# A Fourier transform folded over mirrored positions and computed in turns of the fill-in bank during attention

## What is computed

```python
def fourier_mix(u):
    b, n, _ = u.shape
    uh = u.astype(F32).reshape(b, n, FOURIER_HEADS, HEAD_DIM)
    y = jnp.fft.fft2(uh, axes=(1, 3), norm='ortho').real
    return y.reshape(b, n, GROUP_WIDTH).astype(u.dtype)
...
        y = jnp.concatenate([
            gated_short_conv(a_v, a_b, a_c, conv_w[layer]),
            multiscale_pool(p_in, pool_w[layer], pool_scale[layer]),
            neighborhood_attention(q, k, v, kc, vc, na_rpb[layer]),
            fourier_mix(f_in),
        ], axis=-1)
        x = x + g1 * (y @ w_out[layer])
```

## Time and profile before

| what | value |
|---|---|
| median of three runs | 584.47 us (584.3 to 585.58) |
| the profiled execution | 587.96 us, of which its span 585.8 us |
| busy, PE | 548.4 us (94%) |
| busy, DVE | 447.2 us (76%) |
| busy, ACT | 321.8 us (55%) |
| busy, POOL | 155.8 us (27%) |
| HBM traffic | 160.15 MB read, 17.33 MB written |

### The profile page before, as it was taken

How to read it: one execution, slowest core, us unless ns; L and a number is a source line. 1 busy time by engine, 2 the same in 40 slices (tenths; PEclk the granted TensorE clock), 3 DMA queues, 4 the chain that set the end, 5 groups by cost and what they waited for, 6 DMA issues and landing times.

```text
span 585.8 us, 7662 instructions
## 1 busy us (share of the span) xinstructions
PE 548.4 (94%) x2733; PEld 416.7 (71%) x2733; DVE 447.2 (76%) x592; ACT 321.8 (55%) x399; POOL 155.8 (27%) x141
## 2 busy tenths in 40 slices
PE   1789999999999999979999899999999999999995
PEld 1344874677766877857688688888888888877772
DVE  1347688534576465477899899999999999999867
ACT  4440132354442922255586586676876677866624
POOL 5000743132230510020871321233312333210060
PEclk9799999999999999988999899999999999999998
DMA  8999995759521740149979999999999999999565
GB/s 288 390 371 318 376 379 189 234 158 401 216 73 56 267 145 37 46 153 396 323 291 392 383 345 392 393 392 393 391 388 391 390 390 379 380 383 358 199 223 208
DMA packets 88902, 173.92 MB, mean 297 GB/s; under 512 B 5399, under 2 KB 18907, under 8 KB 88749
## 3 DMA queue, kind: packets, MB, share of 16 engines
q1 hardware_dynamic: 82722, 155.43, 73.9%
q10 hardware_dynamic: 2780, 9.99, 4.2%
q0 software_dynamic: 3376, 8.18, 3.9%
HBM read 160.15 MB, written 17.33 MB: 303 GB/s over the span
## 4 chain that ended last, share of the span: by engine, by line
PE 76%; DMA 8%; DVE 7%; ACT 4%; issue 3%; SPq 1%; POOL 0%; DVEq 0%; ACTq 0%; POOLq 0%
PE psum L897 6%; PE psum L1271 4%; PE psum L1273 4%; PE psum L1244 4%; PE psum L1272 4%; PE psum L1245 4%; PE psum L1246 4%; PE psum L905 4%; PE psum L1255 3%; PE psum L1256 3%; PE psum L1254 3%; DMA w<-in_moe_w 3%; PE psum L942 3%; DMA ada<-in_ada_w 3%; PE psum L944 3%; PE psum L943 3%
## 5 line engine op out<-in xcount | busy, mean ns | idle before, releaser
L2245 DVE TENSOR_TENSOR w_lo<-w,w_hi 128x2048 fp32r<-128x2048 f32 x32 | 72.9, 2282 | 1.2 <-ACT w_hi L1670 1.2
L2234 DVE TENSOR_TENSOR w_lo<-w,w_hi 128x1024 fp32r<-128x1024 f32 (+2 forms) x30 | 68.6, 2292 | 0.0
L1661 ACT CAST w_hi<-w 128x2048 fp32r<-128x2048 f32 x30 | 57.3, 1911 | 15.7 <-PE psum L1256 14.4
L1670 ACT CAST w_hi<-w 128x2048 fp32r<-128x2048 f32 x32 | 60.3, 1917 | 7.2 <-issue 4.1
L2228 DVE TENSOR_TENSOR w_lo<-w,w_hi_a 128x2048 fp32r<-128x2048 f32 (+1 forms) x30 | 51.7, 1760 | 3.2 <-ACT w_hi_a L1649 2.8
L1271 PE MATMUL psum<-w_hi,heT_hi 128*128 128x512 f32 x120 | 50.1, 417 | 0.8 <-DVE w_lo L2245 0.8
L763 POOL COPY idx<-idx 128x1 int32 x12 | 10.4, 870 | 141.5 <-PE psum L1217 141.5
L1852 DVE SCALAR_TENSOR_TENSOR rows<-ada,cc,rows 128x512 f32<-128x512 f32 x48 | 39.5, 825 | 10.6 <-DMA ada<-in_ada_w 9.1
L1273 PE MATMUL psum<-w_hi,heT_lo 128*128 128x512 f32 x120 | 47.5, 396 | 0.0
L1272 PE MATMUL psum<-w_lo,heT_hi 128*128 128x512 f32 x120 | 47.2, 393 | 0.0
L1245 PE MATMUL psum<-w_lo,xgT_hi 128*128 128x512 f32 x120 | 46.8, 390 | 0.0
(11 more groups left out here) (368 smaller groups left out, 1265.1 us busy)
## 6 DMA issues: line engine op xcount, KB each, us to landing
w<-in_moe_w SPq DMA_DIRECT2D x32, 2048.0 KB, 13.6
w<-in_moe_w SPq DMA_DIRECT2D x32, 1024.0 KB, 13.6
ada<-in_ada_w SPq DMA_DIRECT2D x12, 2048.0 KB, 18.7
win<-in_w_in SPq DMA_DIRECT2D x8, 1024.0 KB, 14.5
expert_rows<-ysb ACTq DMA_DIRECT2D x15, 512.0 KB, 6.4
expert_rows<-zero SPq DMA_DIRECT2D x1, 5120.0 KB, 21.4
wout<-in_w_out SPq DMA_DIRECT2D x4, 1024.0 KB, 4.9
x<-in_x SPq DMA_DIRECT2D x2, 1024.0 KB, 10.7
```

The source lines that it names most:

```text
L1670: act.copy(w2_hi[:, :, hs], w2_sb[b][:, :, hs]).then_inc(w2_hi_ok[half], 1)
L2234: v.tensor_tensor(w3_lo[b][:, ks, :], w3_sb[b][:, ks, :], w3_hi[:, ks, :], ALU.subtract).then_inc(w3_lo_ok, n)
L2245: v.tensor_tensor(w2_lo[b][:, :, hs], w2_sb[b][:, :, hs], w2_hi[:, :, hs], ALU.subtract).then_inc(w2_lo_ok[half], 1)
```

## The change

The transform is folded. POOL adds and subtracts mirrored positions once (sums for the cosines, differences for the sines), and then once or twice more, so that even and odd frequencies need only 65, 64, 128, 128 and 127 positions. Over channels PE then has ten matmuls with 128 columns, over positions ten that together have 1024 columns, 512 for each half of the 256 channels. They are done in five turns, where rounds 2 to 6 of the loop put a third half tile or nothing: turns 0 to 2 over channels, turns 3 and 4 over positions. Each turn uses bank 7, so it waits until the tile before is out, and the next tile waits until ACT has copied the turn's result. POOL joins the mirrored outputs into a buffer of their own (`yF`). The third half tiles move to rounds 0, 1 and 7, one half tile falls into round 8, and the pooling matmuls are put before the last `output`.

The quarters of `w_out` are loaded in the order k = 4,5; 6,7; 0,1; 2,3, and ACT rounds the first two in rounds 7 and 8; POOL forms the low parts of these two, DVE of the others. The first projection handles both halves of the first 128 tokens, first with k = 4, 6, 7, 0, 1, then with k = 5, 2, 3. One expert load (the first matrix of expert 1) is issued earlier on SP, after the last tile.

```diff
-        def more_fill(p):
-
-            return p % 2 == 0
+        FOURIER_AT = (2, 3, 4, 5, 6)
+
+        def third(p):
+
+            return p < 2 or p == NP_ - 1
+
+        HI_AT = [3, 4, 5, 6, 2, 7, 0, 1]
+
+        def wout_ks(i):
+
+            return slice(2 * (i ^ 2), 2 * (i ^ 2) + 2)
 
...
+            sp.wait_ge(ada_dve, 5)
+            sp.dma_start(dft_sb[:], dft_seq).then_inc(dft_in, 16)
...
+            load_first(moe_w1, w1_sb, 1, w1_in)
             sp.wait_ge(pool_ps, 2)
             sp.wait_ge(o_copied, 2)
             load_first_w2(1)
-            sp.wait_ge(fn_ok, 2)
-            load_first(moe_w1, w1_sb, 1, w1_in)
...
+            low_w(2)
+            low_w(3)
+
+            def both(dst_sum, dst_dif, a, b):
+
+                gp.tensor_tensor(dst_dif, a, b, ALU.subtract)
+                link(gp.tensor_tensor(dst_sum, a, b, ALU.add))
+
+            gp.wait_ge(pj_act, 2)
+            both(f_sum[:, :, 1:GW], f_dif[:, :, 1:GW], fT[:, :, 1:GW], fT[:, :, GW + 1:N][:, :, ::-1])
+            both(f_sum[:, :, 0:1], f_odd[:, :, 0:1], fT[:, :, 0:1], fT[:, :, GW:GW + 1])
+            both(f_sum[:, :, 1:P], f_odd[:, :, 1:P], f_sum[:, :, 1:P], f_sum[:, :, P + 1:GW][:, :, ::-1])
+            both(f_dif[:, :, 1:P], f_rest[:, :, 0:P - 1], f_dif[:, :, 1:P], f_dif[:, :, P + 1:GW][:, :, ::-1])
+            gp.tensor_tensor(f_half[:], f_sum[:, :, 0:HD], f_sum[:, :, HD + 1:P + 1][:, :, ::-1], ALU.subtract)
+            gp.tensor_tensor(f_sum[:, :, 0:HD], f_sum[:, :, 0:HD], f_sum[:, :, HD + 1:P + 1][:, :, ::-1], ALU.add
+                             ).then_inc(fold_ok, 1)
+            for n in range(4, len(FILL)):
...
+            def mirrored(up_, down, even, odd):
+
+                gp.tensor_tensor(up_, even, odd, ALU.add)
+                return gp.tensor_tensor(down, even, odd, ALU.subtract)
+
+            gp.wait_ge(fn_even, 2)
+            e4, e2, e1 = f_parts[:, :, 0:65], f_parts[:, :, 65:129], f_parts[:, :, 129:257]
+            o1, o2 = f_parts[:, :, 257:385], f_parts[:, :, 385:N]
+            mirrored(yF[:, :, 1:GW:2], yF[:, :, GW + 1:N:2][:, :, ::-1], e1, o1)
+            mirrored(yF[:, :, 2:GW:4], yF[:, :, GW + 2:N:4][:, :, ::-1], e2, o2[:, :, 0:127:2])
+            mirrored(yF[:, :, 4:GW:4], yF[:, :, GW + 4:N:4][:, :, ::-1], e4[:, :, 1:64], o2[:, :, 1:127:2])
+            gp.tensor_copy(yF[:, :, 0:GW + 1:GW], e4[:, :, 0:65:64]).then_inc(fn_copied, 1)
+
+            for i in range(2):
                 gp.wait_ge(wo_hi_ok, i + 1)
                 ks = slice(2 * i, 2 * i + 2)
-                gp.tensor_tensor(wout_lo[:, ks, :], wout[:, ks, :], wout_hi[:, ks, :], ALU.subtract).then_inc(wo_lo_gp, 1)
+                gp.tensor_tensor(wout_lo[:, ks, :], wout[:, ks, :], wout_hi[:, wout_ks(i), :], ALU.subtract
+                                 ).then_inc(wo_lo_gp, 1)
...
+            def fourier(i):
+
+                if i == 0:
+                    pe.wait_ge(consts_in, 112)
+                    pe.wait_ge(fold_ok, 1)
+                if i < 3:
+                    pe.wait_ge(pj_act, 4 + i)
+                    cos, sin = head_dft[:, 0:P], head_dft[:, P:2 * P]
+                    for h in range(2):
+                        mine = ([(f_sum[:, h, 0:HD + 1], cos), (f_half[:, h, :], cos)],
+                                [(f_odd[:, h, :], cos), (f_dif[:, h, 1:P + 1], sin)],
+                                [(f_rest[:, h, 0:P - 1], sin)])[i]
+                        for a, (w, c_) in enumerate(mine):
+                            n = w.shape[1]
+                            m = pe.matmul(bank[7][0:n, a * GW + h * P:a * GW + (h + 1) * P], w, c_,
+                                          start=True, stop=True)
+                    m.then_inc(fd_ok, 1)
+                    return
+                h = i - 3
+                pe.wait_ge(pj_dve, i - 2)
+                pe.wait_ge(fd_copied, 3)
+                pe.wait_ge(dft_in, 16)
+                for a, k, cols_ in ((0, 65, slice(0, 65)), (1, HD, slice(65, 129)), (2, P, slice(129, 257)),
+                                    (3, P, slice(257, 385)), (4, P - 1, slice(385, N))):
+                    m = pe.matmul(bank[7][:, cols_], f_freq[a][0:k, h * P:(h + 1) * P], dft_sb[0:k, cols_], start=True, stop=True)
+                m.then_inc(fn_ok, 1)
...
+                if p == NP_:
+                    pe.wait_ge(d_ok, 1)
+                    for h in range(2):
+                        pe.matmul(bank[2 + h][:], pw[:, h, :], dpool[:, h, :],
+                                  start=True, stop=True).then_inc(pool_ps, 1)
...
-                if more_fill(p):
+                if p in FOURIER_AT:
+                    fourier(FOURIER_AT.index(p))
+                elif third(p):
                     fill(nf)
                     nf += 1
-            while nf < 20:
-                fill(nf)
...
-            for t in range(NT):
-                for h in range(2):
-                    m = pe.matmul(bank[t][:, h * GW:(h + 1) * GW], fT[:, h, t * P:(t + 1) * P], head_dft[:],
...
-                        m = pe.matmul(bank[4 + h][:, cols_], fcs[:, t, h, part * P:(part + 1) * P],
...
+            def project_part(ks, high, low, turned):
+
+                for n in range(2):
+                    cc_ = slice(n * 512, (n + 1) * 512)
+                    tc = slice(0, P)
+                    for k in ks:
+                        if n == 0:
+                            pe.wait_ge(y_hi_ok, high[k][0])
+                            pe.wait_ge(wo_hi_ok, high[k][1])
+                        pe.matmul(bank[n][:], yT_hi[:, HI_AT[k], tc], wout_hi[:, k, cc_], start=(k == 4), stop=False)
+                    for k in ks:
+                        if n == 0:
+                            pe.wait_ge(*low[k])
+                        pe.matmul(bank[n][:], yT_hi[:, HI_AT[k], tc], wout_lo[:, k ^ 4, cc_], start=False, stop=False)
+                    for k in ks:
+                        if n == 0:
+                            pe.wait_ge(y_lo_ok, turned[k])
+                        m = pe.matmul(bank[n][:], yT_lo[:, k, tc], wout_hi[:, k, cc_], start=False, stop=(k == 3))
+                    if ks[-1] == 3:
+                        m.then_inc(wo_ok, 1)
 
             def project_first():
 
...
+                high = {4: (1, 1), 6: (2, 2), 7: (2, 2), 0: (3, 3), 1: (3, 3), 5: (5, 1), 2: (4, 4), 3: (4, 4)}
+                low = {4: (wo_lo_gp, 1), 5: (wo_lo_gp, 1), 6: (wo_lo_gp, 2), 7: (wo_lo_gp, 2),
+                       0: (wo_lo_ok, 1), 1: (wo_lo_ok, 1), 2: (wo_lo_ok, 2), 3: (wo_lo_ok, 2)}
+                turned = {4: 1, 6: 2, 7: 2, 0: 3, 1: 3, 2: 4, 3: 4, 5: 5}
+                project_part((4, 6, 7, 0, 1), high, low, turned)
+                project_part((5, 2, 3), high, low, turned)
...
             project_first()
-            project(1)
             project(2)
...
-                act.wait_ge(pj_dve, 4)
-                act.wait_ge(d_ok, 1)
-                act.wait_ge(stored, 16)
-                act.copy(wout_hi[:, 2 * i:2 * i + 2, :].rearrange("p k n -> p (k n)"),
+                act.wait_ge(*((fn_copied, 1), (fn_copied, 1), (pj_dve, 3), (pj_dve, 4))[i])
+                act.copy(wout_hi[:, wout_ks(i), :].rearrange("p k n -> p (k n)"),
...
+                    act.wait_ge(fn_ok, i - 2)
+                    act.wait_ge(d_ok, 1)
+                    act.copy(f_parts[:, i - 3, :], bank[7]).then_inc(fn_even, 1)
...
+                if p == NP_:
+                    high_wout(1)
...
+                if p in FOURIER_AT:
+                    fourier_copy(FOURIER_AT.index(p))
+                elif third(p):
+                    nf += 1
+                    if done < len(FILL) and nf >= 2 * (done + 1):
+                        tile_done(done)
+                        done += 1
+                if p == NP_ - 1:
+                    act.wait_ge(o_copied, 1)
+                    high_y(4, 1)
+                    high_wout(0)
+                    high_y(6, 2)
...
+            high_y(0, 2)
             high_wout(2)
+            act.wait_ge(pool_ok, 2)
+            high_y(2, 2)
+            act.wait_ge(o_copied, 2)
+            high_y(5, 1)
             high_wout(3)
...
+            late = {(3, 0): pool_pairs, (3, 1): pool_fours, (4, 0): pool_eights, (4, 1): lambda: pool_means(0),
+                    (5, 0): lambda: pool_means(1), (5, 1): lambda: (conv_in(0), pool_less()),
+                    (6, 0): lambda: conv(0), (6, 1): lambda: conv_in(1), (7, 0): lambda: conv(1),
+                    (7, 1): lambda: conv_out(0), (8, 0): lambda: conv_out(1)}
...
+            low_y(1, 4, 1)
+            low_y(2, 6, 2)
+            low_y(3, 0, 2)
+            low_wout(2)
+            head_pair(1)
+            low_y(4, 2, 2)
+            low_y(5, 5, 1)
+            low_wout(3)
...
+    seq = np.zeros((P, N))
+    seq[0:65, 0:65] = cos[0:65, 0:257:4]
+    seq[0:64, 65:129] = cos[0:64, 2:256:4]
+    seq[:, 129:257] = cos[0:P, 1:256:2]
+    seq[:, 257:385] = sin[1:P + 1, 1:256:2]
+    seq[0:127, 385:N] = sin[1:P, 2:256:2]
```

(36 more changed lines are left out.)

130 lines of the change are left out of this document (41 added, 89 removed).

## The result

The changed kernel takes 582.1 us (median of 7 runs, 581.39 to 583.82), the kernel before 586.88 (7 runs, 584.3 to 587.82; three of them are those of the table before, the four new ones took 586.88 to 587.82). The ratio of the means is 0.9931, with a 95% interval of 0.9908 to 0.9954: **faster, by 4.0 us (2.7 to 5.4)**, or 0.7%. A second measurement later gave 582.1 again, ratio 0.9943 (0.9922 to 0.9964). The profiled execution took 582.48 us, its span 580.2 us.

A forecast was written before the change was run, and what follows sets the result against it. PE, busy 94% of the span, was taken as the bound. Terms -5.9 - 3.0 - 2.1 + 5.1 + 1.5 = -4.4 us, from the median 584.47 to 580.1 us; range 576.5 to 582.8 us.

The forecast's parts named there:

- turns on PE: Ten channel matmuls at 2.45 us and a position part at 1.83 us added to PE, together 4.3 us.
- waits in the loop: PE's waits for ACT's two copies (0.81 + 0.68 us) and for DVE (1.5 us) covered by moved work: -3.0 us.
- Fourier rows gone: The old channel and position transforms removed from PE's tail: 3.45 + 6.72 = 10.17 us.
- old waits of the first part: Idle time in the old first projection part, 7.57 us where its matmuls need 5.46, all gone: -2.1 us.
- new waits: First projection part, after the last `output` ends (Z): PE idle 1.9 us for ACT and 3.2 for DVE, +5.1 us.
- clock: One stretch of PE at the lower clock level around the tail's new idle time: +1.5 us of 0 to 3.4.
- rival C: A longer stretch at the lower clock, or one more wait at seams without room: 582.1 us; chance 0.12.
- the prediction's own sign: Projection of the second 128 tokens starts 5.9 (at full clock) or 4.4 us earlier than 216.7, else the step is wrong.
- The hold: In the tail, POOL's work on `w_out` keeps DVE's low parts of yT from starting until Z + 1.6.
- Rival B: DVE isn't held by POOL in low yT: 2.0 of 3.2 us go, 576.6 us with the clock high; chance 0.12.
- Rival A: PE's clock stays high behind the tail's new gaps: -5.9 us, 578.6 us; chance 0.22.
- Nothing on POOL or in the loop became late: POOL's fold (6.6 us, 7 with waits) and joining (3.4 us), and the turns' new waits in the loop, costed at nothing.

The follow-up runs named there:

- pool_one_quarter: The changed kernel with DVE instead of POOL forming the low part of the second quarter of `w_out`: 579.61 us, ratio 0.9897 to the kernel before.

## Where the prediction failed, and where it held

**The step that failed is the price of the turns on PE: +4.3 us in the sum, 6.4 in the traces.** The sum still came to 4.4 us less, and the traces show 4.3 less from the first scores to `project(2)`, because a second term was off the other way, the waits in the loop. That was luck:

| term | forecast | in the traces |
|---|---|---|
| Fourier rows gone | -10.2 | -10.2 |
| turns on PE | +4.3 | +6.4 |
| waits in the loop | -3.0 | -4.6 |
| old waits of the first part | -2.1 | -2.1 |
| new waits | +5.1 | +4.6 |
| clock | +1.5 | +1.6 |
| sum | -4.4 | -4.3 |

The time, 582.1 us, is 2.0 above the forecast of 580.1 and within the range. The forecast stood on a median of three runs, 584.47; every later median of the kernel before lies between 585.8 and 586.9. 0.9931 of 584.47 is 580.4. That 582.1 is also rival C's number is chance: its cause is in neither trace of the changed kernel. And the prediction's own sign, `project(2)` 4.4 us ahead of 216.7, isn't met as it is written: it starts 5.71 ahead, at 210.99, 1.41 of which were there before the first scores.

- **The turns.** "The position part has 1024 columns in all, like the two pooling matmuls" priced ten small matmuls by their columns, 1.83 us. They took 3.19. A matmul of 64 columns has the price of one of 128, 0.222 us, so they cost ten times 0.222, plus 0.2 for each turn, plus 0.57 for their shapes. The channel part, priced by count (2.45), was short only by its shapes and turns (3.18). Of the 2.1 us missed in both parts, columns instead of count make 0.4; the larger pieces are what the five turns cost once each (1.0) and the unequal shapes (0.9), both put at nothing. The router's 0.245 us a matmul was 0.2 too much in all.
- **The waits in the loop.** Round 8 had no half tile before (the 20 were used up by round 7), so PE stood idle there for ACT's copies. Scores to Z is 93.63 us before and 97.24 - 6.37 - 1.81 = 89.06 after, so 4.57 us went, where the notes had been added up to 3.0. One small note (0.22 us, for ACT's `up`) was left out; the rest fits the five waits costing some 0.26 us more than their notes: an idle note starts when the matmul ahead ends (0.39 us shown, 0.23 apart), and the first behind a wait is slower (0.47 us). That split is worked out, not isolated, and it stands on one trace of the kernel before; scores to Z of the variants differ by up to 1.2 us through notes of that size.
- **The new waits.** Each was where and for whom it was forecast. The notes are 1.68 and 2.24 us, forecast 1.9 and 3.2. The third high quarter came at Z + 2.65 (forecast 2.5), the low one at Z + 6.28 (forecast 6.9): POOL took 4.58 us for a quarter, not 4.9, and was done at Z + 1.2.
- **The hold** was as the earlier trace rows had suggested: 4.21 us against 0.69. Rival B was wrong. Where the hold was taken away (pool_one_quarter) what B had priced came about: a shorter wait and a clock that stays high, 3.0 us in all.
- **The clock.** Rival A was wrong. By the rule of the Trainium skill (TensorE: Matmul & The Clock Gate, "Why this matters for your kernels": no idle gaps over about 3 us) no fall was due, for no gap reached 3 us. The traces disagree: the clock was 0.50 from 201 to 204 us behind gaps of 1.68 and 2.24. Rival C's longer stretch didn't come in the two traces of the changed kernel, but did in five variants of it, in three of them behind the same two gaps.
- **Nothing on POOL or in the loop became late**, as costed; what PE gained went through, with 369.1 and 369.2 us from `project(2)` to the end. So the expert load that SP issues earlier shows no effect of its own.

## What to carry to other kernels

Work that is taken off the bottleneck engine also uncovers what the other engines did behind it: here the kernel with the fold gained nothing when their work wasn't moved ahead, or when PE's order didn't follow what becomes ready. Price small matmuls by count and not by columns, and add something for each separate group and for weights of unequal shape. And count a short wait on PE at more than its note, with the clock that may fall behind it: taking two waits with notes of 3.9 us out of the way gave 5.8.
